# A transformer block in fp32: where the weights and the moving rows of the projections and the FFN lie in SBUF

## What is computed

```python
h = rmsnorm(x, g_mix_pre)
z = h @ w_in                                  # [2048, 1024] @ [1024, D_IN], 33 column blocks of 128 when padded
o_a = nsa_mixer(...)                          # compressed, selected and windowed attention, 6 heads
o_b = dilated_mixer(...)                      # three dilated windows, 4 heads each
o_c = banded_attention(..., sinks)            # sliding window with sinks, 6 heads
mix = concat([o_a, o_b, o_c]) @ w_out         # [2048, 1024] @ [1024, 1024]
x = x + rmsnorm(mix, g_mix_post)
u = causal_conv3(rmsnorm(x, g_ffn_pre) @ w_up) + conv_b       # [2048, 1024] @ [1024, 5632]
a, b = split(u)
x = x + rmsnorm((gelu(a) * b) @ w_down, g_ffn_post)           # [2048, 2816] @ [2816, 1024]
```

## The kernel before the change

| tile | role | byte | modulo 512 |
|---|---|---|---|
| `idt` | moving rows of the transposes | 16512 | 128 |
| `h_hi`, `h_lo` | moving rows of project | 19872, 85408 | 416 |
| `z_xs` | rows transposed by `L458`; buffer of the FFN weights | 167552 | 128 |
| `z_w_raw` | landing place of w_in | 196288 | 192 |
| `z_w_hi`, `z_w_lo` | weights of project | 204480, 212672 | 192 |
| `low` | moving rows of the up product | 19872 | 416 |
| `k0_hi`, `k0_lo`, `qm`, `vs` | ring slots 0 to 3 | 52640 to 85535 | 416 |
| `f_own` | ring slots 4 and 5 | 85536 | 32 |
| `f_g_hi`, `f_g_lo` | weights of the down product | 120736, 165792 | 416 |
| `p_w_hi`, `p_w_lo` | moving rows of mix_out | 106016, 138784 | 32 |
| `p_ot`, `p_oh`, `p_ol` | rows and weights of mix_out | 179776, 196160, 204352 | 64 |

## Time and profile before

### The profile page before, as it was taken

One profiled execution on the slowest core, in us unless ns is written; L12 is line 12 of the kernel. 1 busy time (PEld: TensorE's weight loads), 2 busy tenths in 40 slices (PEclk: granted clock), 3 DMA queues, 4 the chain that ended last, 5 costly groups with the idle time before them and its releaser, 6 DMA issues. The chain is left out here.

```text
span 3500.6 us, 45326 instructions
## 1 busy us (share of the span) xinstructions
PE 3392.4 (97%) x16530; PEld 2707.0 (77%) x16530; DVE 1386.8 (40%) x3825; ACT 1161.2 (33%) x1979; POOL 569.4 (16%) x503
## 2 busy tenths in 40 slices
PE   8999999997998999999989999999999999999998
PEld 6888888886777866666658878887888788888886
DVE  5111101105666776666655444403440244115421
ACT  5111111115665755445443333302330233113310
POOL 1556654430000012232010000000000000000000
PEclk9999999998999999999999999999999999999999
DMA  5789965657888732342126775566556655665553
GB/s 193 262 306 321 319 241 201 214 181 182 200 196 204 178 97 54 81 98 55 56 81 207 231 283 192 191 238 233 192 192 240 229 192 191 238 227 204 191 192 141
DMA packets 299252, 676.02 MB, mean 193 GB/s; under 512 B 99392, under 2 KB 154944, under 8 KB 284864
## 3 DMA queue, kind: packets, MB, share of 16 engines
q1 hardware_dynamic: 265344, 517.80, 46.0%
q0 software_dynamic: 33696, 155.40, 12.4%
HBM read 495.93 MB, written 185.57 MB: 195 GB/s over the span
## 5 line engine op out<-in xcount | busy, mean ns | idle before, releaser
L1299 PE MATMUL a_ot_ps<-a_turned_w,vs 128*65 128x256 f32 (+3 forms) x1452 | 448.4, 420 | 1.2 <-issue 1.2
L525 PE MATMUL z_banks<-h_hi,z_w_hi 128*128 128x512 f32 x972 | 387.4, 399 | 0.0
L525 PE MATMUL z_banks<-h_lo,z_w_hi 128*128 128x512 f32 x972 | 384.6, 396 | 0.0
L525 PE MATMUL z_banks<-h_hi,z_w_lo 128*128 128x512 f32 x972 | 384.5, 396 | 0.0
L1577 PE MATMUL banks<-low,f_own 128*128 128x512 f32 x1344 | 320.4, 398 | 12.4 <-issue 6.2
L1577 PEld LDWEIGHTS banks<-low,f_own 128*128 128x128 f32 x1344 | 255.6, 190 | 73.0 <-issue 13.5
L1372 ACT ACTIVATE w_small<-w_small,a_negm 128x128 f32<-128x128 f32 (+3 forms) x510 | 247.0, 518 | 163.2 <-DVE a_negm L1451 98.9
L1299 PEld LDWEIGHTS a_ot_ps<-a_turned_w,vs 128*65 128x65 f32 x1452 | 179.5, 139 | 82.4 <-issue 69.9
L1451 DVE CUSTOM_DVE_ANT_0 w_small<-a_s_ps,near 128x128 f32<-128x128 f32 (+2 forms) x456 | 169.1, 394 | 168.3 <-PE a_s_ps L1263 140.1
L525 PEld LDWEIGHTS z_banks<-h_lo,z_w_hi 128*128 128x128 f32 x972 | 182.7, 188 | 43.8
L525 PEld LDWEIGHTS z_banks<-h_hi,z_w_lo 128*128 128x128 f32 x972 | 182.8, 188 | 42.6
(11 more groups left out here) (241 smaller groups left out, 6530.9 us busy)
## 6 DMA issues: line engine op xcount, KB each, us to landing
f_own<-f_hi SPq DMA_DIRECT2D x88, 512.0 KB, 3.6
f_own<-f_lo SPq DMA_DIRECT2D x88, 512.0 KB, 4.5
z_xs<-in_w_ffn POOLq DMA_DIRECT2D x33, 1024.0 KB, 8.3
f_hi<-z_v_hi POOLq DMA_DIRECT2D x33, 1024.0 KB, 4.9
f_lo<-z_xs POOLq DMA_DIRECT2D x33, 1024.0 KB, 5.6
low<-z_hi SPq DMA_DIRECT2D x48, 512.0 KB, 7.6
k_hi<-f_hi SPq DMA_DIRECT2D x44, 512.0 KB, 3.6
k_hi<-f_lo SPq DMA_DIRECT2D x44, 512.0 KB, 4.5
```

What stands on the lines that cost most here:

```text
L525: last = pe.matmul(banks[:, 4 * k + n, :], w[:, k, c, :], h[:, c, tok], start=(c == 0 and q == 0), stop=(c == DC - 1 and q == 2))
L1299: last = pe.matmul(ot_ps[0:out_width(g), at:at + count * P], values, rows, start=(x == 0), stop=(x == len(blocks) - 1), skip_group_check=True)
```

## The change

It moves tiles. No instruction is added, removed or put in another order on any engine: all five queues hold the same rows as before.

```diff
@@ project
+LANE = 128
+        sb("pad", [P, (LANE - (8 * (HD + 1) * 4 + CMP // 2 + 8) % LANE) % LANE])
+        w_hi = sb("w_hi", [P, 2, DC, P], F32R)
+        w_lo = sb("w_lo", [P, 2, DC, P], F32R)
+        w_raw = sb("w_raw", [P, 2, DC, P])
         xs = sb("xs", [P, 4, D])
...
-        w_raw = sb("w_raw", [P, 2, DC, P])
-        w_hi = sb("w_hi", [P, 2, DC, P], F32R)
-        w_lo = sb("w_lo", [P, 2, DC, P], F32R)
@@ mix_out
-        eps = sb("eps", [P, 1])
         ot = sb("ot", [P, 2, D])
...
         st = sb("st", [P, 2, 8])
+        eps = sb("eps", [P, 1])
@@ ffn
+        sb("pad", [P, LANE - 2 * NT * (HD + 1) % LANE])
         own = sb("own", [P, RING - AHEAD, 2, D], F32R)
+        g_hi = sb("g_hi", [P, NF, QT], F32R)
+        g_lo = sb("g_lo", [P, NF, QT], F32R)
...
-        g_hi = sb("g_hi", [P, NF, QT], F32R)
-        g_lo = sb("g_lo", [P, NF, QT], F32R)
```

## The result

The changed kernel takes 3465.24 us, the median of three runs (3464.02 to 3466.08), against 3507.08 us before (3504.13 to 3512.5): a ratio of 0.9878, 95% interval 0.9856 to 0.9900. That is 1.2% faster, and clear of the 0.2% that a measurement here can tell. The profiled execution took 3465.24 us (span 3463.4), 37.2 us less than that of before, where 38.8 were forecast. One more run of each kernel is left out as far slower than all the others (4839.34 us before; 5829.33 us after, at a granted clock of 0.63).

The account below looks back on a forecast made before the run. PE's own stream was taken as the bound, busy 97% of the span. Savings of 21.1 + 7.6 + 5.0 + 5.1 = 38.8 us took the profiled 3502.5 to 3463.7, giving a forecast median of 3468 us, range 3460 to 3482.

Parts of the forecast that it names:

- The reading of the profile: PE is busy 97% of the span; only time per matmul can change, 227 ns at equal places, otherwise 232 to 233.
- Project: In project, 3168 matmuls go from 233.3 to 226.7 ns each, all on the path: 21.1 us less.
- FFN: Matmuls on `f_own`: up product 7.6 us less over 28 visits, down product 5.0 us less over 16 visits.
- mix_out: In mix_out, 768 matmuls go from 233.3 to 226.7 ns at equal place 32: 5.1 us less.
- the bounds: In mix_out, the gain is 0 if only place 416 is good, 5.1 us if equality counts; 5.1 was taken.
- Transposes and elementwise work at nothing: Transposes whose rows move from 128 to 416 change by 0, at most 0.9 us; elementwise work on moved tiles 0.
- Supply: In project, GpSimd's splits keep 12.1 us of margin, less than 1 taken; DMA rises to 0.93; neither comes due.
- The rival with slower DMA: In project, moved tiles losing 64-byte starts lengthen DMA packets, making DMA the bound; 3532 us at 50% longer; chance 0.02.

Follow-up runs that it names:

- `aligned`: Changed kernel plus every tile PE reads in project, attend, mix_out and FFN at 416 modulo 512, except the value tile; 3468.45 us, ratio 0.9894 to the kernel before.
- `far`: Changed kernel with weights and moving rows pulled apart: project 256 and 64 bytes, mix_out 256, FFN's own slots 256 and 480; 3487.36 us.
- `project_alone`: Kernel before with the change made in project only, mix_out and FFN as before; 3485.06 us, ratio 0.9943.

## Why the prediction was right, step by step

1. **The reading of the profile.** That only the time per matmul could move, and that the same instruction with tiles at equal places took 227 and otherwise 232 to 233 ns, was right in each of the four roles. So was taking start-to-start times and not durations, though here the durations fell by about as much, 6 to 8 ns.
2. **Project**, 21.1 us forecast, 17.8 measured: the one term clearly mis-sized. From 100 to 500 us it is as forecast, 226.7 ns. Both traces hold the same 3456 matmuls in the same order, so the shortfall of 3.3 us can be read pair by pair. From 500 us on, where PE also transposes the values, 1.4 us are missing: the 34 matmuls before a transpose stay at 232.9 and 232.8 ns, and of those behind one the first takes 316 ns in both and the next five go from 232.5 to 231.6 only, while from the seventh on it is 233.3 to 226.7. Another 0.35 us are missing in the same way between 40 and 100 us. (The step multiplied all 3168 by one number from a stretch without transposes.) The last 1.5 us lie before 40 us. The first 12 matmuls ran longer at 1.2 GHz in this execution and took 30.48 - 26.07 = 4.41 us against 28.66 - 25.13 = 3.53, and the first transposes took 0.4 us more; these aren't the layout's, as far as the traces tell.
3. **FFN**, 7.6 + 5.0 = 12.6 forecast, 13.5 measured. Every visit of 48 away from a stall is now 10.88 us; read pair by pair, the matmuls on `f_own` gave 7.5 + 4.9 us, and the 28 of them that are slow in one trace or both, behind a wait or at the low clock, 0.3. The other 0.8 us, which the steps didn't count, come from slots that were matched before: the matmuls next to `f_own` had been slowed too (the seams above).
4. **mix_out**, 5.1 forecast, 4.8 measured (212.23 to 207.47 us). The choice between the bounds, that equality counts and not the place 416, is shown by this row, by `aligned` and by `far`.
5. **Transposes and elementwise work at nothing**: right; eight transposes take 1.03 us with `z_xs` at 416 against `idt` at 128, as with both at 128, and DVE, ACT and POOL are within 1 us of before.
6. **Supply**: right. PE has no wait on weights in project; the share of DMA rose to 0.92, and GpSimd waits 82.5 us instead of 70.3 for its own loads, with room for it. The rival with slower DMA had one count wrong: a column block moves 6.8 MB (60.4 MB from 300 to 500 us) and not some 5, so the moved places carry 60% of it and not 70%. Nothing came of it: a load into `z_w_raw` lands after 5.2 us instead of 5.0, one into `z_xs` after 8.5 instead of 8.3.

The sum missed by 1.6 us in the profiled execution; the median came out 2.8 us under the forecast. That the sum is so close is in part luck: project fell short by 3.3 us, the FFN gave 0.9 more, and attend was 1.7 us shorter (967.0 to 965.3), which the change doesn't explain, as with the same tiles it took 969.8 us in `project_alone`.

What the prediction said beyond its numbers was partly wrong. It showed that equality modulo 128 is not enough and left 256 and 512 open, while the change is written for 512; 256 does the same. And the trace before did hold 24 matmuls of project (before a transpose) at equal places with 232 ns, which `aligned` confirms: the rule doesn't reach a matmul under which a transpose's weights load, nor the half dozen behind a transpose.

The rule of the Trainium skill on two independent read ports ("TensorE: Matmul & The Clock Gate", "Step-by-step: what each phase is for") doesn't hold for this stream: the same matmul takes 226.7 or 233.3 ns by where the weights that load under it lie. It takes the higher clock to see it. At 1.2 GHz the matmuls on `f_own` take 427 ns in both layouts (15 before, 13 after). Half of that, 213.3 ns, is an estimate of what 512 columns need at 2.4 GHz, and both layouts lie above it, by 13.3 and 20 ns. Whether the 13.3 ns are due to the load as well isn't shown, as no run leaves the loads out.

Why the places matter is not settled. Shown is that it depends on both places modulo 256 bytes, that it begins in the matmul under which the weights load and can last into the next few, and that its sign turned between 512 and 256 columns; a mechanism behind it would be a guess.

## What to carry to other kernels

When one instruction form has two durations in a profile, compare the addresses of its operands; a ring of slots in tiles of different stages is a ready-made experiment. In a stream of fp32 matmuls of 512 columns that each load weights of their own, put weights and moving rows at the same place modulo 256 bytes, all of them, since one displaced tile of two gives the gain back; here it was 2.9% per matmul and 1.2% of the kernel for two pads of under 400 bytes and another order of tiles. Don't expect it next to transposes, and measure again at other widths: at 256 columns it was 1.7 ns per matmul worse.

## What the runs showed of the hardware that I had not expected

- The period is 256 bytes, not 512 (`far`: 226.7 ns at 256, 233.3 at 64).
- Distances of 4 to 16 bytes are erratic: 232.4, 230.7 and 233.2 ns above, 233.2 and 228.4 at 4 and 16 below, and 236.6 at 4 below with the roles swapped.
- Means over a stream are steady to a fraction of a nanosecond: three matched matmuls take 680 ns in project, mix_out and the FFN, with DMA busy at 0.58 or at 0.92 of its time, and three at a distance of 32 or 64 bytes some 700 (697 at 128). Single matmuls at a distance aren't steady: 228 to 241 ns.
- A displaced load under every third matmul makes that one 239.3 ns and the group no faster than with all three displaced; the delay lasts into matmuls under which only matched weights load.
- At the low clock the places make no difference: 427 ns in either layout.
- With 256 columns the sign turns: 120.0 ns matched, 118.3 unmatched.
